# Expert weights in transfers of two ring places, features dealt in twos, and the first expert's gather split between its slots

## What is computed

```python
def ec_moe(h, w_router, w_gate, w_up, w_down):
    bsz, n_tok, d = h.shape
    cap = EC_CAPACITY_FACTOR * n_tok // N_EXPERTS
    aff = jax.nn.softmax(jnp.einsum('btd,de->bte', h, w_router).astype(jnp.float32), axis=-1)
    gate, idx = lax.top_k(jnp.swapaxes(aff, 1, 2), cap)
    xs = jax.vmap(lambda hb, ib: hb[ib])(h, idx)
    hid = (jax.nn.silu(jnp.einsum('becd,edf->becf', xs, w_gate))
           * jnp.einsum('becd,edf->becf', xs, w_up))
    y = jnp.einsum('becf,efd->becd', hid, w_down) * gate[..., None].astype(h.dtype)
    return jax.vmap(lambda yb, ib: jnp.zeros((n_tok, d), y.dtype).at[ib.reshape(-1)].add(yb.reshape(-1, d)))(y, idx)
```

## Time and profile before

| | us |
|---|---|
| median of 3 runs | 2693.76 |
| the three runs | 2693.76, 2693.76, 2706.36 |
| the profiled execution | 2698.98 |
| its span | 2697.2 |
| PE busy in the span | 2159.6 |
| DVE busy | 599.1 |
| ACT busy | 339.7 |
| POOL busy | 95.3 |

### The profile page before, as it was taken

How to read it: one execution, slowest core, us unless ns; L and a number is a source line. 1 busy time by engine, 2 the same in 40 slices (tenths; PEclk the granted TensorE clock), 3 DMA queues, 4 the chain that set the end, 5 groups by cost and what they waited for, 6 DMA issues and landing times.

```text
span 2697.2 us, 36720 instructions
## 1 busy us (share of the span) xinstructions
PE 2159.6 (80%) x16332; PEld 1248.3 (46%) x16332; DVE 599.1 (22%) x1136; ACT 339.7 (13%) x673; POOL 95.3 (4%) x107
## 2 busy tenths in 40 slices
PE   5999998555566566667888865587999999989999
PEld 1444674222123222233554422273676884756874
DVE  1121554001011011111322210065533000641000
ACT  2101222000010000011111000031342000222000
POOL 0001000000000000000111100000120000100000
PEclk7999998999999999999999999988999999989999
DMA  8633606999999999999999999943632453313451
GB/s 334 254 127 141 232 17 238 423 425 424 425 424 421 422 425 415 421 406 424 424 424 424 424 424 425 414 157 122 219 127 89 147 196 119 128 43 110 147 204 38
DMA packets 158911, 755.27 MB, mean 280 GB/s; under 512 B 12249, under 2 KB 75737, under 8 KB 102050
## 3 DMA queue, kind: packets, MB, share of 16 engines
q1 hardware_dynamic: 158754, 752.92, 70.3%
HBM read 751.83 MB, written 1.05 MB: 279 GB/s over the span
## 4 chain that ended last, share of the span: by engine, by line
PE 55%; DMA 39%; DVE 3%; ACT 2%; issue 1%; POOL 0%; DVEq 0%; SPq 0%; ACTq 0%; POOLq 0%
DMA ring<-w_up_dram 14%; PE psum L648 11%; DMA ring<-w_gate_dram 11%; DMA ring<-w_down_dram 9%; PE psum L550 8%; PE psum L676 5%; DMA ring<-hyb_w_dram 4%; PE psum L1171 3%; PE psum L462 2%; PE psum L1541 2%; PE psum L1235 2%; PE psum L441 2%; PE psum L1279 2%; PE psum L1377 1%; PE psum L1010 1%
## 5 line engine op out<-in xcount | busy, mean ns | idle before, releaser
L1171 PE MATMUL psum<-ring,arena 128*32 128x320 f32 x4096 | 360.9, 469 | 280.5 <-DMA ring<-w_gate_dram 141.4
L1171 PEld LDWEIGHTS psum<-ring,arena 128*32 128x32 f32 x4096 | 112.0, 111 | 440.6 <-DMA ring<-w_up_dram 170.4
L648 PE MATMUL psum<-arena,ring 128*128 128x256 f32 x1408 | 306.8, 381 | 0.0
L1235 PE MATMUL psum<-ring,arena 128*32 128x512 f32 x1344 | 210.3, 602 | 108.6 <-DMA ring<-w_down_dram 108.5
L648 PEld LDWEIGHTS psum<-arena,ring 128*128 128x128 f32 x1408 | 269.4, 191 | 37.0
L550 PE MATMUL psum<-ring,arena 128*128 128x512 f32 x480 | 214.6, 609 | 10.2 <-ACT arena L2719 8.5
L1235 PEld LDWEIGHTS psum<-ring,arena 128*32 128x32 f32 x1344 | 47.5, 109 | 246.0 <-DMA ring<-w_down_dram 171.6
L550 PEld LDWEIGHTS psum<-ring,arena 128*128 128x128 f32 x480 | 93.1, 196 | 129.1 <-issue 129.1
L2305 DVE TENSOR_TENSOR arena<-arena,psum 128x320 f32<-128x320 f32 (+1 forms) x32 | 16.7, 521 | 581.4 <-PE psum L1171 575.5
L676 PE MATMUL psum<-ring,arena 128*128 128x512 f32 x288 | 125.0, 596 | 0.0
L1180 PE MATMUL psum<-ring,arena 128*32 128x64 f32 x2048 | 119.9, 291 | 0.0
(11 more groups left out here) (371 smaller groups left out, 2110.0 us busy)
## 6 DMA issues: line engine op xcount, KB each, us to landing
ring<-w_gate_dram SPq DMA_DIRECT2D x128, 1376.0 KB, 18.1
ring<-w_up_dram SPq DMA_DIRECT2D x128, 1376.0 KB, 18.1
ring<-w_down_dram SPq DMA_DIRECT2D x112, 1536.0 KB, 19.9
ring<-w_mod_dram SPq DMA_DIRECT2D x72, 1024.0 KB, 5.1
ring<-w_ffn_in_dram SPq DMA_DIRECT2D x88, 512.0 KB, 5.1
ring<-w_ffn_out_dram SPq DMA_DIRECT2D x14, 1536.0 KB, 7.1
ring<-w_in_dram SPq DMA_DIRECT2D x16, 1024.0 KB, 5.6
ring<-hyb_w_dram SPq DMA_DIRECT2D x10, 1024.0 KB, 16.8
```

What stands on the lines that cost most here:

```text
L648: ins = nc.tensor.matmul(b[:, i * 256:(i + 1) * 256], ws[k // 4][:, k % 4, u, i * P:(i + 1) * P], R(XT + k * 256, 256), start=(k == 0), st ...
L1171: ins = nc.tensor.matmul(banks[u][c][32 * j:32 * j + 32, 0:GMAIN], R(XST + k * HALF + e * CAP, CAP), w3[:, 64 * c:64 * c + 64, QGROUP * j: ...
L1235: ins = nc.tensor.matmul(ybanks[half][32 * c:32 * c + 32, :], stationary, w, start=((half, c) not in begun), stop=(unit >= 36), skip_group ...
```

## The change

1. *Ring.* `enlist(key, wide=True)` gives a piece two neighbouring places, beginning at an even one (an odd place is skipped). SP waits for the later of the pieces that held the two. Of six places three wide pieces fit.
2. *Gate and up.* A piece holds two features a partition: 128 x 5504 floats, 2752 KB, eight pieces an expert instead of 16. Partition `p` of pair `j` holds features 256`j` + 2`p` and the next, one contiguous stretch of 22016 bytes in memory.
3. *Features dealt in twos.* To match, the gather takes every second column, and the modulation's columns (`shsc`, `modcol`) are dealt in the same way by eight small matmuls into a new PSUM result `dealt`.
4. *Down.* Pieces of 6, 5, 5 and 5 groups of rows (`DOWN_ROWS`) instead of seven of 3.
5. *The steps beside* are still taken one per piece: eight and three `next` instead of 16 and six.
6. *Gather.* `gather(0)` and `gather(1)` come ahead of the first gate piece, the other features two by two behind the gate pieces of expert 0, in banks 6 and 7.
7. *Router.* The product of the first token tile moves between the tiles of the transpose, that of the second between parts 2 and 3 of `w_mod`; ACT's exponential takes the bias and the sum itself, and some small DVE operations fall away or move.

```diff
+DOWN_ROWS = ((0, 6), (6, 11), (11, 16), (16, QROWS))
...
-        def enlist(key):
-            n = len(order)
+        def enlist(key, wide=False):
+            n = places_taken[0] + (wide and places_taken[0] % 2)
...
+            taken = [(n + i) % RING for i in range(2 if wide else 1)]
+            tenant_before[key] = [latest[i] for i in taken if latest[i] is not None]
+            for i in taken:
+                latest[i] = key
+            places_taken[0] = n + len(taken)
...
+            def between_tiles():
+                last_modulation(range(2))
+                route(0)
+
+            scaled_T("x2", after_first=between_tiles)
+            last_modulation(range(2, 3))
+            route(1)
+            last_modulation(range(3, 4))
...
-                for k in range(KT):
-                    if e == 0:
-                        pe.wait_ge(bank_drained[bank_of(("xs", k))], nth(("xs", k)))
-                    if e % 2 == 0 and k == (4 if e == 0 else 0):
+                for pair in range(KT // 2):
+                    if e == 0 and pair == 0:
+                        gather(0)
+                        gather(1)
+                    if e % 2 == 0 and pair == (2 if e == 0 else 0):
                         scatter_rows(e)
                     for u in range(2):
-                        enlist(("expert", e, u, k))
...
+                        enlist(("expert", e, u, pair), wide=True)
+                        pe.wait_ge(slot_loaded[slot_of(("expert", e, u, pair))], count_of[("expert", e, u, pair)])
+                        for i in range(2):
+                            k = 2 * pair + i
...
+                        if e == 0 and u == 0 and pair < KT // 2 - 1:
+                            gather(2 * pair + 2)
+                            gather(2 * pair + 3)
                         next(beside, None)
...
-                for s in range(7):
-                    enlist(("down", e, s))
+                for s, (r0, r1) in enumerate(DOWN_ROWS):
+                    enlist(("down", e, s), wide=True)
...
-                    if s < 6:
+                    if not last_slot:
                         next(beside, None)
...
-            def weights_in(key, *parts):
-                n = order[key]
-                if n >= RING:
-                    freed, times = freed_by[by_order[n - RING]]
+            def weights_in(key, *parts, wide=False):
+                n = slot_of(key)
+                if tenant_before[key]:
+                    freed, times = freed_by[max(tenant_before[key], key=lambda earlier: order[earlier])]
                     s.wait_ge(freed, times)
```

More of the change, by code:

```diff
@@ L219, in program @@
         affinity_exp = semaphore("affinity_exp")
+        affinity_max = semaphore("affinity_max")
         pads_zeroed = semaphore("pads_zeroed")
@@ L911, in last_modulation, with route @@
                     modulation_part("mod2_0", 2, k, 6)
[L913 to L917, removed]
+            def route(t):
+                if t == 0:
+                    b = next_bank("router")
+                    if nth("router") > 1:
+                        pe.wait_ge(bank_drained[bank_of("router")], nth("router") - 1)
                 for k in range(KT):
@@ L936, in _ @@
                     ins.then_inc(bank_filled[bank_of("affT")], 1)
+            b = next_bank("dealt")
+            if nth("dealt") > 1:
+                pe.wait_ge(bank_drained[bank_of("dealt")], nth("dealt") - 1)
+            mc = modcol[:, :].rearrange("p (m c) -> p m c", c=2)
+            for n, per_feature in enumerate((shsc[:, 8:16], mc[:, 24:32, 0])):
+                for i in range(2):
+                    for half in range(2):
+                        ins = nc.tensor.matmul(b[64 * half:64 * half + 64, 8 * n + 4 * i:8 * n + 4 * i + 4],
+                                               const("ident").rearrange("p (q i) -> p i q", i=2)[:, i, :],
+                                               per_feature.rearrange("p (j h) -> p h j", h=2)[:, half, :], start=True,
+                                               stop=True, skip_group_check=True)
+                        if n == i == half == 1:
+                            ins.then_inc(bank_filled[bank_of("dealt")], 1)
             last_modulation(range(4, KT))
@@ L1230, in _ @@
                 unit, begun = 0, set()
+                halves = [0, 1] + [half for r0, r1 in DOWN_ROWS for half in range(2) for r in range(r0, r1)]
+                final = {(half, n % 4): n for n, half in enumerate(halves)}
                 def down_unit(half, stationary, w):
@@ L1235, in down_unit @@
                     ins = nc.tensor.matmul(ybanks[half][32 * c:32 * c + 32, :], stationary, w,
-                                           start=((half, c) not in begun), stop=(unit >= 36), skip_group_check=True)
+                                           start=((half, c) not in begun), stop=(unit == final[half, c]), skip_group_check=True)
                     begun.add((half, c))
@@ L2876, in _ @@
             a.wait_ge(normed_second_ready, tally.gave(normed_second_ready))
-            a.wait_ge(bank_drained[bank_of("router")], nth("router"))
-            a.activation(sm(0, 32), sm(0, 32), ACT.Exp).then_inc(affinity_exp, 1)
-            a.wait_ge(affinity_exp, tally.gave(affinity_exp))
+            a.wait_ge(affinity_max, tally.due(affinity_max))
+            for t in range(TT):
+                ins = a.activation(sm(t * 16, 16), result("router")[:, t * 16:(t + 1) * 16], ACT.Exp, bias=sm(32 + t, 1),
+                                   accum_out=sm(34 + t, 1))
+                if t == 0:
+                    ins.then_inc(affinity_exp, 1)
+                else:
+                    ins.then_inc(bank_drained[bank_of("router")], 1)
             keep_rows("mod2_0", 2)
```

132 lines of the change are left out of this document (72 added, 60 removed).

## The result

| | before | changed |
|---|---|---|
| median of 4 runs, us | 2693.76 | 2772.39 |
| lowest and highest, us | 2690.74, 2706.36 | 2769.48, 2781.37 |
| ratio, 95% interval | | 1.0271 [1.0239, 1.0303] |
| the profiled execution, us | 2698.98 | 2773.61 |
| its span, us | 2697.2 | 2771.8 |

The change makes the kernel slower, as forecast, but by 78.6 us of the medians (by the ratio 73, between 64 and 82) and not by 39.7; the time lies above the predicted range.

A forecast was written before the change was run, and what follows sets the result against it. The prediction took the expert-weight stream as the bound. Its terms, 46.4 + 12.5 - 13 - 7.2 + 1.0 = +39.7 us, on 2693.8 gave 2733.5 us, range 2704 to 2756.

The forecast's parts named there:

- experts 10 to 13: Context solve steps 9 to 15 bunch before the combine, freeing the down place late: 11.6 us stall, four times, +46.4 us.
- experts 5 to 9: Context load between gate and up frees its place late for the next up piece: 2.5 us stall, five times, +12.5.
- plain experts: Experts without context work: queued loads cover PE for 20.2 us, place reloads by 14.8, spare 5.4 us, no stall.
- bytes' time: Weight loads: longer rows, 1408 fewer on each engine at 9.2 ns a row, -13 us; bounds nothing and -26.
- hole at the start: Empty stretch in the first expert's loads closes because PE gathers only two features first: -7.2 us.
- first wide loads: First double load needs two freed places, mod parts 2 and 3; start left unchanged, bounds 0 to +1.7 us.
- the end: Behind the last landing PE has five down rows to multiply instead of three: +1.0 us.
- bound from below for the stalls: Experts 10 to 13 with hand-overs at nothing: block 8.8 us, stall 5.4, sum +21.5 us.
- rival 2: Cheap hand-overs and restarts: block 8.8 us, restart 0.93, stalls sum 21.1, total +2, 2696 us; chance 0.10.
- Rival 1: The ring of weight places covers all of PE's absences, no stall anywhere: 2674.6 us; chance 0.06.
- Rival 3: Plain experts stall too, three large pieces being a coarser buffer: 2 us in each of twelve, +24, 2757 us; chance 0.08.
- Rival 4: Long rows gain nothing in the weight loads: +13 us, 2746 us; chance 0.14.

The follow-up runs named there:

- experiment 5: The kernel of experiment 3, but all eight features gathered ahead of the first gate piece, as before the change: 2687.53 us, ratio to the kernel before 0.9960.
- experiment 1: The changed kernel, but experts 10 to 13 take a context step after each feature's weights again: 2700.77 us, ratio to the kernel before 0.9981.
- experiment 4: The kernel before, narrow places and old transfers, but a context step only behind every second feature's weights: 2755.3 us, ratio to the kernel before 1.0177.
- experiment 7: The changed kernel plus three unused identity matmuls after each step of the block in experts 10 to 13: 2755.13 us, ratio to the kernel before 1.0229.
- experiment 3: The changed kernel with both step edits, per feature in experts 10 to 13 and twice per piece in 5 to 9: 2685.55 us, ratio to before 0.9924.
- experiment 6: The kernel of experiment 3, but each gate or up piece loaded by two transfers with 11008-byte rows: 2693.0 us, ratio to the kernel before 0.9986.
- 2: The changed kernel, but experts 5 to 9 take two context steps behind each wide piece: 2756.44 us, ratio to the kernel before 1.0185.

## Why the prediction was right and wrong

Windows of the changed kernel around the block (columns as before; PEclk is the number behind the five engines):

```profile
1322.00:1330.20 8.20, 5.76 (x71) 4.30 (x70) 1.38 (x2) 0.59 (x1) 1.27 (x2) 1.00 1.02 429
1331.60:1334.20 2.60, 2.60 (x34) 1.20 (x25) 0.00 (x0) 0.00 (x0) 0.00 (x0) 0.50 1.06 454
...
1336.70:1349.80 13.10, 6.68 (x48) 5.69 (x48) 5.21 (x8) 3.38 (x5) 0.00 (x0) 0.95 0.89 382
1349.80:1354.60 4.80, 3.94 (x16) 3.34 (x16) 1.38 (x2) 0.00 (x0) 0.00 (x0) 0.50 0.00 0
1354.60:1360.20 5.60, 5.60 (x10) 2.45 (x10) 4.07 (x7) 0.00 (x0) 0.00 (x0) 0.63 0.00 0
```

Two lines of the changed kernel's timeline of PE, down pieces of a plain expert; in the earlier trace rows such a piece waited for 1.8 us:

```profile
514.47 4.26 PE L1277 MATMUL psum<-ring,arena 128*32 128x512 f32 x20 [3.35 <-DMA ring<-w_down_dram]
520.99 2.77 PE L1277 MATMUL psum<-ring,arena 128*32 128x512 f32 x20 [2.25 <-DMA ring<-w_down_dram]
```

Step by step, in us:

| step of the prediction | forecast | measured |
|---|---|---|
| experts 10 to 13 | +46.4 | +72.2 |
| experts 5 to 9 | +12.5 | +18.4 |
| plain experts | 0 | +3.4, expert 2 alone |
| bytes' time | -13 | -13 by the landings |
| hole at the start | -7.2 | gone; 7.5 before, 6.2 in experiment 5 |
| first wide loads | 0 (bound +1.7) | about +1 |
| the end | +1.0 | not measured apart |

By the landings: an unbroken stream brings a wide gate or up piece every 6.55 us where two narrow ones took 2 x 3.31, and four down pieces in 25.6 where seven took 25.8; over 128 and 16 of them that is 13 us. The second wide piece landed at 454.9, the fourth narrow one at 453.6.

The three misses in the stalls add up to 25.8 + 5.9 + 3.4 = 35.1 us; the span missed the forecast by 74.6 - 39.7 = 34.9. That the two agree to 0.2 us is luck: behind the last landing the changed kernel's profile is 2.2 us shorter than the one before, with no reason in the change.

**Right: the mechanism.** That the large transfers take places from the context's steps, that steps 9 to 15 fall into a block ahead of the combine and that the six-row piece then comes free too late for the queue: experiment 1 takes it away by the steps' cadence, experiment 4 makes it without the transfers. Experts 0, 1, 3, 4, 14 and 15 have no gap. The restart costs 8.5 - 6.1 = 2.4 us (the prediction's 5.8 - 3.31 is 2.5, not 2.4). Expert 11's period, fourth down piece to fourth down piece, is 1473.7 - 1374.6 = 99.1 us, longer than the 91 forecast by about the same miss. The rate is 428 to 429 GB/s in the slices without a stall, 1% over 424 to 425, and 1% of 1305 us is the 13 forecast; packets fell from 158911 to 133566. The bound from below for the stalls (+21.5) and rival 2, which rested on it, were far off.

**Wrong: the size of "experts 10 to 13".** This is the step that failed: the stall of 11.6 us, four times, was 18.1 on average. It took each duration from the kernel before, whose rows stand at a clock of 1.00, and put its hand-overs at 0.7 us for ACT and 0.8 for DVE. For expert 10 the parts came to:

| part | forecast | measured |
|---|---|---|
| last up piece | 3.0 | 4.0 |
| step 8 | 2.0 | 2.3 |
| block | 15.0 | 18.1 |
| combine and transposes | 5.8 | 7.8 |
| six down rows | 3.64 | 3.63 |

The windows above say where it went. From 1331.6 to 1334.2 and from 1349.8 to 1354.6 the granted clock is 0.50, the lower of TensorE's two levels, 1.2 of 2.4 GHz. The Trainium skill, "TensorE: Matmul & The Clock Gate", section "What's actually happening", names the same two levels. Before the first fall PE had been busy for 5.76 of 8.20 us, and the rest was its wait for the up piece. Before the second it had been busy for 6.68 of 13.10 us, in short bursts between hand-overs, at a clock of 0.95. The combine behind it ran at 0.63 on average. So an L1208 group of 16 takes 2.13 instead of 1.4, the later matmuls of the block 1.98 and 2.07 for 1.1 and 1.2, the combine 5.64 instead of 3.70. Experts 11 to 13 have such rows too (combines of 5.52, 4.93 and 5.20 us).

In the block each hand-over took 0.8 to 0.9 us, and a small DVE instruction (L2299, 0.50) had been left out. Added up for expert 10, PE's own rows are longer by 1.0 (piece), 0.3 (step 8), 1.9 (block) and 1.9 (combine), together 5.1 us, and PE's waits inside the block are 7.5 us where 6.2 were reckoned: 1.3.

Experiment 7 tests the first part: with PE kept at work 14.6 of the 25.8 us go, and the combine's row, 3.60 us at a clock of 1.00, says that it is the clock that came back. What stays is 57.6 - 46.4 = 11.2. In its expert 10, which is late by 13.6, all else is as long as forecast; the block takes 16.9 us for 15.0, of which 0.7 is the last filling (up to 1339.72 above, behind a step that ended at 1339.03) and the rest hand-overs and the omitted instruction. In its experts 11 and 13 the last up piece still fell into a slower stretch (rows of 2.02 and 2.36 us for 1.37). The step gave 2 us a block as its upper bound, and never allowed for a slower PE.

**Wrong: the size of "experts 5 to 9".** The first three came in at 2.7 to 3.2 for 2.5. The last two are at 5.2 and 4.6. In expert 8, the first of these, PE multiplied the up piece ahead of the second context step in 2.36 us and 1.73 (row at 1119.98 above) where 1.36 is full clock, and gave the place back 8.1 us after that piece had landed. Experiment 1 has the same code there; its two rows take 1.37 and 1.36 us, the place came back after 6.8, and the load was late by 3.7. So most of what expert 8 lost beyond that is the clock; no run was made for it.

**Wrong: "plain expert, no stall".** The spare of 5.4 us was right for experts without a step of their own between combine and transposes. Expert 2 has one, and it was read as plain. That step alone does not make the stall: in experiments 3, 5 and 6, with the same step, the fourth down piece of expert 2 comes in time, in experiment 1 it is 0.5 us late, in 2 and 7 1.8 and 1.9. The combine and the first down rows of expert 2 take 3.88 and 1.07 us in the changed kernel and 3.70 and 0.62 in experiment 3. It is the step and the lower clock together that use up the spare.

**The rivals.** Rival 1, the ring covers all, and 2, cheap hand-overs, fall with the dips. Rival 3 holds for expert 2 alone. Rival 4, no gain from long rows, falls by the rate and experiment 6. The chance of slower, 0.84, was well placed; the range was too narrow on its high side. Its end of 2756 is what rival 4 (+13) and the whole of the upper bounds (+7.6 and +1.7) give, half of them would be 2751; but either way the bound itself knew no change of clock.

## What to carry to other kernels

When pieces of a stream are merged, ask what else was dealt out one per piece: the side work loses its gaps, and what overflows becomes a chain of hand-overs that must end before the next place comes free. Here the change had some 20 us to gain, 13 of them by the coarser pieces, and the lost places cost 90; a `next` for each feature, and a second one behind context pieces, kept the gain (2685.55 us, ratio 0.9924). Durations that are moved to a place where an engine idles between short bursts should be priced at its lower clock too, as the upper bound at least.

## What was not expected of the hardware

In plain experts PE does the same matmuls at the same rate of the stream, and yet the granted clock from 500 to 800 us is 0.80 in the change and 0.97 before. What differs is the shape of PE's waits: 1.3 to 1.8 us for each narrow piece, 2.3 to 3.4 us for each wide one (the rows at 514 and 520 us above). Of the two kernels with narrow pieces, one bunches its steps (experiment 4) and keeps 0.96; all with wide pieces have 0.80 to 0.84, with long rows or short ones. Where the stream sets the pace no cost of it shows: experiment 3 has the shortest stream of all at 0.82. It costs where PE is what the queue waits for, here some 15 us in four blocks, and there matmuls without a purpose bought it back (experiment 7). No run changed the waits alone, so that they are the cause is a reading of these rows and no more.
